# Two ScalarE casts of layer two move behind the squares at the boundary between two layers

## What is computed

```python
x = x + rms_norm(mixer(rms_norm(x, g[0])), g[1])
x = x + rms_norm(swiglu(rms_norm(x, g[2]), w_gate_up, w_down), g[3])
```

## Time and profile before

| | |
|---|---|
| median of 3 runs | 799.12 us (798.79 to 801.34) |
| profiled execution, its own time | 798.64 us |
| its span (first to last instruction) | 797.0 us |
| TensorE matmul rows busy | 783.8 us, 98% |
| VectorE busy | 504.0 us, 63% |
| ScalarE busy | 379.9 us, 48% |
| mean DMA rate | 170 GB/s |

### The profile page before, as it was taken

One profiled execution on the slowest core, in us unless ns is written; L12 is line 12 of the kernel. 1 busy time (PEld: TensorE's weight loads), 2 busy tenths in 40 slices (PEclk: granted clock), 3 DMA queues, 4 the chain that ended last, 5 costly groups with the idle time before them and its releaser, 6 DMA issues.

```text
span 797.0 us, 12927 instructions
## 1 busy us (share of the span) xinstructions
PE 783.8 (98%) x4789; PEld 688.4 (86%) x4789; DVE 504.0 (63%) x640; ACT 379.9 (48%) x460; POOL 62.4 (8%) x76
## 2 busy tenths in 40 slices
PE   8999999999999998999999999999999999999997
PEld 7999978888888886999999999999988888888885
DVE  6788987765645545876747557567547756555453
ACT  5665667443344334835545435445357433343331
POOL 2000002100000000321202202111002000000000
PEclk9999999999999999999999999999999999999999
DMA  8544654776455555368466455564622874555601
GB/s 237 171 118 123 232 187 162 240 266 207 158 180 188 192 188 150 81 173 223 111 185 170 126 165 145 145 189 134 237 82 78 282 268 163 172 196 181 223 18 53
DMA packets 158817, 135.45 MB, mean 170 GB/s; under 512 B 5192, under 2 KB 149184, under 8 KB 158784
## 3 DMA queue, kind: packets, MB, share of 16 engines
q1 hardware_dynamic: 157312, 130.75, 52.1%
q0 software_dynamic: 1376, 4.22, 2.4%
q10 hardware_dynamic: 96, 0.04, 0.0%
HBM read 133.91 MB, written 1.07 MB: 169 GB/s over the span
## 4 chain that ended last, share of the span: by engine, by line
PE 94%; DVE 2%; ACT 1%; DMA 1%; issue 1%; SPq 0%; POOL 0%; DVEq 0%; POOLq 0%; ACTq 0%
PE ps L1042 19%; PE ps L1044 19%; PE ps L1043 19%; PE ps L1048 8%; PE ps L1050 8%; PE ps L1049 8%; PE ps L1323 2%; PE ps L1313 2%; PE ps L1292 1%; PE ps L1188 1%; PE ps L1119 1%; PE ps L1286 1%; PE ps L1063 1%; DMA raw<-in_w_qkv_a 1%; PE ps L1130 1%
## 5 line engine op out<-in xcount | busy, mean ns | idle before, releaser
L662 DVE TENSOR_TENSOR w_lo<-raw,w_hi 128x2048 fp32r<-128x2048 f32 (+2 forms) x144 | 277.4, 1946 | 35.0 <-ACT w_hi L423 33.6
L423 ACT ACTIVATE w_hi<-raw 128x2048 fp32r<-128x2048 f32 (+2 forms) x144 | 232.4, 1637 | 56.7 <-DMA raw<-in_w_kv_b 19.5
L1042 PE MATMUL ps<-w_hi,xt 128*128 128x512 f32 x352 | 139.5, 396 | 0.0
L1044 PE MATMUL ps<-w_hi,xt 128*128 128x512 f32 x352 | 137.4, 390 | 0.0
L1043 PE MATMUL ps<-w_lo,xt 128*128 128x512 f32 x352 | 137.1, 390 | 0.0
L546 ACT ACTIVATE work<-ps,stat 128x256 f32<-128x256 f32 x44 | 21.0, 477 | 198.8 <-PE ps L1044 198.8
L1048 PE MATMUL ps<-xt,w_hi 128*128 128x256 f32 x384 | 110.2, 287 | 0.7 <-DVE w_lo L942 0.7
L1049 PE MATMUL ps<-xt,w_hi 128*128 128x256 f32 x384 | 108.6, 283 | 0.0
L1050 PE MATMUL ps<-xt,w_lo 128*128 128x256 f32 x384 | 108.6, 283 | 0.0
L1042 PE MATMUL ps<-w_hi,ot 128*128 128x512 f32 x240 | 94.9, 396 | 0.0
L1044 PE MATMUL ps<-w_hi,ot 128*128 128x512 f32 x240 | 93.7, 391 | 0.0
(11 more groups left out here) (128 smaller groups left out, 1095.5 us busy)
## 6 DMA issues: line engine op xcount, KB each, us to landing
raw<-in_w_gate_up SPq DMA_DIRECT2D x88, 512.0 KB, 4.7
raw<-in_w_kv_b SPq DMA_DIRECT2D x96, 256.0 KB, 3.6
raw<-in_w_down SPq DMA_DIRECT2D x22, 1024.0 KB, 4.9
raw<-in_w_q_b SPq DMA_DIRECT2D x48, 256.0 KB, 3.7
raw<-in_w_qkv_a SPq DMA_DIRECT2D x23, 512.0 KB, 4.9
raw<-in_w_o_a SPq DMA_DIRECT2D x4, 1024.0 KB, 5.4
raw<-in_w_o_b SPq DMA_DIRECT2D x4, 1024.0 KB, 4.9
work<-in_norm_gains POOLq DMA_DIRECT2D x4, 512.0 KB, 5.2
```

The source lines that it names most:

```text
L423: act.activation(w_hi[:, s % CUT, 0:size(s)], raw[:, s % RAW, 0:size(s)], ACT.Copy).then_inc(hi_made, 1)
L662: dve.tensor_tensor(w_lo[:, c, 0:n], raw[:, s % RAW, 0:n], w_hi[:, c, 0:n].bitcast(F32), ALU.subtract).then_inc(lo_made, 1)
L1042: mm(out, xs[0], ws[0], start=start, stop=False)
L1044: return mm(out, xs[1], ws[0], start=False, stop=stop)
```

## The change

ScalarE casts B0+4 not ahead of the squares of the output, but behind the first sum of squares of x, where B0+5 was cast. It casts B0+5 behind the second sum of squares of x. No other engine's instructions change.

```diff
             swiglu(0, FA0, [B0 - 1, B0, B0 + 1])
-            for u in range(2, 5):
-                hi(B0 + u)
+            hi(B0 + 2)
+            hi(B0 + 3)
 
             square_h(1, 0, B0 - 1)
             square_h(1, 1, B0 - 1, [0])
...
             cut_x(2, 0, 6, xkv, 8, range(4, 8))
             square_x(1, 0)
-            hi(B0 + 5)
+            hi(B0 + 4)
             cut_x(2, 1, 4, xkv, 8)
             value_b(0, 0, 0)
             square_x(1, 1)
+            hi(B0 + 5)
             cut_x(2, 0, 6, xt, 4)
             value_b(0, 0, 1)
             cut_x(2, 1, 4, xt, 4)
```

## The result

The changed kernel took 794.52 us (median of 4, 794.02 to 795.19) against 799.75 us for the kernel before (median of 4, one run more than the three shown ahead of the prediction, 798.79 to 801.34): 5.23 us less, a ratio of 0.9933 (95% interval 0.9917 to 0.9950).

What follows compares the result with a forecast made beforehand. TensorE was taken as the bound, except a 4.5 us wait for `xn` behind a cast awaiting a transfer. Gains accumulated from 4.62 through 5.20 to 5.35 us, with casts costing 0: 799.12 - 5.35 = 793.8, range 792.9 to 796.0.

Steps and rivals of the forecast that it cites:

- Step 1: Layer boundary, ScalarE: first square of the output starts at 311.60 in place of 316.28, 0.04 us after its matmul.
- Step 2: Layer boundary, TensorE: transposes of the new x start at 314.80 instead of 319.42, gain 4.62 us, stall gone.
- Steps 3 and 4: Start of layer two: first V matmul at 317.12, gain 5.20 us; transposes of second token half at 320.33, gain 5.35.
- step 4: Second token half's transposes: TensorE's path gives 320.32, the cuts and update path 320.38; 320.33 taken, gain 5.35 us.
- rival B: Boundary: TensorE's clock falls all the same, 0.6 us lost, 794.4, or 797.6 if six V steps run low; chance 0.05.
- Steps 5 and 6: ScalarE, start of layer two: moved cast of B0+4 stays hidden; B0+5's adds 1.40 us there but costs 0.
- rivals A and D: Start of layer two: A, B0+5's cast not hidden, 795.2, chance 0.05; D, its load late, for example 802.1, chance 0.03.
- The cover of B0+6: Layer two: cast of B0+6 done by 334.15, its VectorE subtraction due at 334.51, 0.36 us to spare.
- Rival C: Layer boundary: the square is held by something else, no gain for TensorE, 799.1; chance 0.04.
- Step 7: Rest of layer two: TensorE has no other such wait behind 328.06, so the 5.35 us gain is kept to the end.

Runs made afterwards that it cites:

- b5_only: Kernel before with only the cast of B0+5 moved, behind the second sum of squares of x: 799.82 us against 799.75 (ratio 1.0002).
- b4_between: Changed kernel with the cast of B0+4 between the output squares of token halves 0 and 1: 795.75 us, ratio 0.9947 to the kernel before.
- fill4: Changed kernel plus four unused ScalarE copies of a token half of x before the first square: 795.65 us, ratio 0.9946 to the kernel before.
- b4_only: Kernel before with only the cast of B0+4 moved, B0+5 left, both behind the first sum of squares of x: 795.33 us against 799.75 (ratio 0.9941).

## Why the prediction was right

It was right: 793.8 was forecast, between 792.9 and 796.0, and 794.52, 793.75 and 792.96 were measured in three comparisons. Of the 0.7 us by which the first lies above the forecast, 0.63 is the base: a fourth execution moved the median of the kernel before from 799.12 to 799.75. The gain was forecast at 5.35 and came out at 5.23.

- **Step 1, the square.** Forecast 0.04 us behind its matmul, measured the same. VectorE's busy time did not delay the update, which started at 314.91 (314.90 was forecast, with the offset) after a wait for GpSimd.
- **Step 2, the transposes.** Forecast at 314.80 with no stall, measured 315.76 less the offset of 0.97, so 314.79.
- **Steps 3 and 4.** The V product and the second transposes came at the forecast times to 0.01 us after the offset. In step 4 the number is a little luckier than the working: the prediction held the two paths for level, but VectorE's update started at 320.27, 0.28 before the forecast, and TensorE's own path decided. The new wait for `xkv` was 0.57 us in place of about 0.7. The low clock did not come, so rival B fell in this kernel. The rule of the Trainium skill (TensorE: Matmul & The Clock Gate, Part 4, PE-mode transpose), that transposes do not bring the full clock about, changed nothing here: two groups of four ran between 315.76 and 317.52 and the granted clock stayed at 1.00.
- **Steps 5 and 6, the two casts.** Hidden, as forecast; rivals A and D fell. The cover of B0+6, the tightest at 0.36 us, held with about 0.6. No run let a cover fail, so its price of 1.40 is not shown. The runs add what was not priced: without B0+5's move the cast of B0+4 alone makes the boundary 0.9 us longer.
- **Rival C.** The square was held by nothing else.
- **Step 7, that the gain is kept to the end.** The size bears it out within what the medians can tell; the argument does not hold. It rested on a list of waits from one execution, in which no wait for the copy stood; the same kernel, profiled again, has it. The two profiled executions differ by 3.5 us and not by 5.4, because this wait and the start each moved by about 1 us, as they do between executions of one kernel.
- **The size.** The boundary gave 5.43 in the two profiles, where 5.35 was forecast. The medians gave 5.2, 6.0 and 6.4. The unchanged boundary took 36.89 to 37.37 in four profiles and the changed one 31.63 to 31.66, so the boundary itself explains 5.2 to 5.7. The rest of the spread is within the scatter of the medians: the three 95% intervals are 4.0 to 6.6, 4.7 to 7.8 and 5.3 to 7.8 us, and 5.43 lies in each.

## What to carry to other kernels

When an engine works through a hand-written order, look at each instruction that waits for a transfer and ask what queues behind it: the cost of the wait is that of the most urgent thing in the queue, here a 0.6 us square at the head of a chain for the busiest engine. Move such an instruction behind the last step of the chain, and check where it lands in turn, since two casts in a slot for one cost 0.9 us. A forecast for a kernel whose executions differ by 1 us is best made stretch by stretch between two points that both versions pass, and the list of waits should be taken from more than one execution before a place is called free.

## What the runs showed of the hardware that was not expected

- The time at the lower clock after nearly the same stall varied. In the kernel before, with 4.46 us of idle, the clock was at 0.50 from 319.0 to 322.5; in b5_only, with 4.19, it was there from 317.9 to 324.7, twice as long. The boundary was only 0.28 us longer. Some 2.1 us of that stretch fell into the idle, which ended at 320.06, and the idle itself was 0.27 us shorter because the load of B0+4 had landed earlier. So the longer stretch cost about 0.5 us, an estimate from these rows, and much less than half of its extra 3.4 us.

```profile
318.00:319.00 1.00, 0.00 (x0) 0.00 (x0) 0.98 (x2) 0.75 (x4) 0.64 (x2) 0.50 1.20 293
...
323.00:324.00 1.00, 1.00 (x5) 1.00 (x4) 1.00 (x3) 0.83 (x5) 0.64 (x2) 0.50 0.00 0
324.00:325.00 1.00, 1.00 (x5) 1.00 (x5) 0.59 (x3) 1.00 (x3) 0.22 (x1) 0.65 0.00 0
```

- A wait of 2.24 us could bring the clock down (b4_between, where about 1.5 us of the boundary are put down to it), while waits of 1.23 us (fill4) and 1.14 us (b4_only) left it at 1.00. The other executions of b4_between were 1.4 to 3.4 us faster than the profiled one. Its long start can explain about 1 us of that (306.28 against 304.5 to 305.6), so the clock perhaps did not always fall; no trace shows it.
- The start up to the last swiglu step varied from 304.3 to 306.3 us over 14 profiles, with the same instructions in front, before any place that the versions differ in.
